# Uneven token parts in the plain dense products of a hybrid decoder layer

## What is computed

```python
z = rmsnorm(x, g_mix_norm) @ w_in             # 2048 -> 8728 columns
u, v, q, kvc, kvs, kvw, g_nsa, g_a, g_b = split_in(z)
o_a = spatial_gate(gelu(u), rmsnorm(gelu(v)))  # 8 groups, causal 128x128 mixing
o_b = nsa(q, kvc, kvs, kvw)                    # compressed + selected + window attention
mix = sigmoid(g_a) * (o_a @ w_proj_gmlp) + sigmoid(g_b) * (o_b @ w_proj_nsa)
x = x + mix @ w_out
hm = rmsnorm(x, g_mlp_norm)
y = x + square(relu(hm @ w_up)) @ w_down
```

## Time and profile before

| | before |
|---|---|
| median of 3 runs | 2601.99 us |
| lowest, highest | 2601.18, 2602.23 us |
| profiled execution, first to last instruction (span) | 2600.4 us |
| TensorE matmuls busy | 2588.5 us, 21487 matmuls |
| weight loads busy | 2560.1 us |
| VectorE, ScalarE, GpSimd busy | 1953.5, 1405.3, 458.6 us |
| granted TensorE clock | 1.00 |
| DMA | 378.79 MB, 146 GB/s on average |

### The profile page before, as it was taken

How to read it: one execution, slowest core, us unless ns; L and a number is a source line. 1 busy time by engine, 2 the same in 40 slices (tenths; PEclk the granted TensorE clock), 3 DMA queues, 4 the chain that set the end, 5 groups by cost and what they waited for, 6 DMA issues and landing times. The chain is left out here.

```text
span 2600.4 us, 57446 instructions
## 1 busy us (share of the span) xinstructions
PE 2588.5 (100%) x21487; PEld 2560.1 (98%) x21487; DVE 1953.5 (75%) x2897; ACT 1405.3 (54%) x2415; POOL 458.6 (18%) x629
## 2 busy tenths in 40 slices
PE   9999999999999999999999999999999999999998
PEld 8999999999999999999999999999999999999998
DVE  6456646668777764455688888888888888898888
ACT  6445436556454442222366666666566665666656
POOL 2001350001121110023202121121121211112113
PEclk9999999999999999999999999999999999999999
DMA  6633552214344344434336575665766756657568
GB/s 212 203 114 114 164 173 74 66 50 132 125 142 137 123 163 138 132 128 145 118 114 159 149 182 144 169 158 149 174 149 167 169 144 166 156 160 175 140 169 180
DMA packets 125325, 378.79 MB, mean 146 GB/s; under 512 B 14258, under 2 KB 15922, under 8 KB 124944
## 3 DMA queue, kind: packets, MB, share of 16 engines
q1 hardware_dynamic: 69328, 245.36, 28.3%
q0 software_dynamic: 52704, 126.25, 22.5%
q10 hardware_dynamic: 3168, 5.45, 0.6%
HBM read 292.29 MB, written 91.00 MB: 147 GB/s over the span
## 5 line engine op out<-in xcount | busy, mean ns | idle before, releaser
L2762 DVE TENSOR_TENSOR w_lo<-w_raw,w_hi 128x1024 fp32r<-128x1024 f32 x351 | 428.0, 1222 | 105.9 <-ACT w_hi L1892 104.5
L1892 ACT ACTIVATE w_hi<-w_raw 128x1024 fp32r<-128x1024 f32 x352 | 370.9, 1062 | 203.0 <-PE aux L1365 69.8
L2069 DVE TENSOR_TENSOR w_lo<-w_raw,w_hi 128x512 fp32r<-128x512 f32 x280 | 202.3, 724 | 340.3 <-ACT w_hi L1510 339.7
L1365 PE MATMUL aux<-at_t,w_hi 128*128 128x260 f32 x2304 | 416.7, 282 | 0.2
L1510 ACT ACTIVATE w_hi<-w_raw 128x512 fp32r<-128x512 f32 x280 | 175.3, 628 | 411.5 <-PE mm L943 391.2
L943 PE MATMUL mm<-a_hi,w_hi 128*128 128x260 f32 x1728 | 357.5, 288 | 0.0
L1365 PEld LDWEIGHTS aux<-at_t,w_hi 128*128 128x128 f32 x2304 | 354.9, 188 | 0.7 <-DVE w_lo L2762 0.3
L1429 PE MATMUL aux<-fb_mid,w_hi 128*128 128x260 f32 x1920 | 352.1, 283 | 1.4 <-DVE w_lo L2762 1.1
L943 PE MATMUL mm<-a_hi,w_lo 128*128 128x260 f32 x1728 | 347.9, 283 | 0.0
L943 PE MATMUL mm<-a_lo,w_hi 128*128 128x260 f32 x1728 | 347.2, 282 | 0.0
L1365 PE MATMUL aux<-at_t,w_lo 128*128 128x260 f32 x1152 | 325.4, 282 | 0.0
(11 more groups left out here) (483 smaller groups left out, 5827.9 us busy)
## 6 DMA issues: line engine op xcount, KB each, us to landing
w_raw<-in_w_ff SPq DMA_DIRECT2D x256, 512.0 KB, 3.5
w_raw<-in_w SPq DMA_DIRECT2D x142, 512.0 KB, 3.5
out_y_t<-y_mid POOLq DMA_DIRECT2D x120, 520.0 KB, 8.0
w_raw<-in_w_st SPq DMA_DIRECT2D x56, 512.0 KB, 3.6
g_in<-merge_d POOLq DMA_DIRECT2D x16, 520.0 KB, 4.9
merge_d<-z POOLq DMA_DIRECT2D x18, 260.0 KB, 4.0
st_f<-in_x_p POOLq DMA_DIRECT2D x8, 520.0 KB, 4.5
pages<-in_cache_cmp POOLq DMA_DIRECT2D x16, 256.0 KB, 4.1
```

The source lines that it names most:

```text
L1365: last = pe.matmul(dst, w, at_t[:, j, e:e + HT], start=FRESH[b] and j == 0 and part == 0, stop=j == KP - 1 and part == 2, skip_group_check ...
L1892: run(hi_of(p, k), source(p, k), ACT.Copy).then_inc(ff_hi, 1)
L2069: dve.tensor_tensor(w_lo[:, c, :], raw(u, c), w_hi[:, c, :].bitcast(F32), ALU.subtract).then_inc(lo_split, 1)
L2762: dve.tensor_tensor(lo_of(p, k), source(p, k), hi_of(p, k).bitcast(F32), ALU.subtract).then_inc(ff_lo, 1)
```

## The change

The tokens of a plain unit are no longer always cut at column 260. A function of the unit's number gives the cut: 260 for units 0 to 3, 256 for 4 to 19, 232 for 20 to 23, 208 for 24 to 27, 260 for 28 to 39, and 256 for 40 to 71 (those of the hardware loops, whose number isn't a Python integer, among them). The first part is written to the last columns of its bank, up to column 511, and the second to the first columns of the next bank, so the 520 sums lie in one run over two banks that are neighbours. VectorE's reads take that run as two pieces of 260 columns. As before, each of a pair's matmuls loads the same weights for itself.

```diff
-        def pair(v):
-            return mm[:, 2 * v:2 * v + 2, 0:HT]
+        def cut_of(n):
+
+            if type(n) is not int or n >= U_PROJ:
+                return 256
+            return HT if n < U_KV else 256 if n < U_VU else 232 if n < U_VU + 4 else 208 if n < U_VU + 8 else HT
+
+        def pair(v, n):
+            o = (2 * v + 1) * 512 - cut_of(n)
+            return mm[:, :, :].rearrange("p b n -> p (b n)")[:, o:o + TOK].rearrange("p (a b) -> p a b", a=2)
+
+        def column_parts(v, n):
+            cut = cut_of(n)
+            return ((mm[:, 2 * v, 512 - cut:512], slice(0, cut)), (mm[:, 2 * v + 1, 0:TOK - cut], slice(cut, TOK)))
...
                         for w, a, part in ((wh, ah, 0), (wh, al, 1), (wl, ah, 2)):
-                            for h in range(2):
-                                last = pe.matmul(mm[:, 2 * v + h, 0:HT], w, a[:, kt, h * HT:(h + 1) * HT],
+                            for dst, cut in column_parts(v, n):
+                                last = pe.matmul(dst, w, a[:, kt, cut],
                                                  start=first and k == 0 and part == 0,
                                                  stop=final and k == CK - 1 and part == 2)
...
-                dve.tensor_tensor(halves(dst), pair(u[1]), halves(rstd[:, :]), ALU.mult).then_inc(mm_read, 1)
+                dve.tensor_tensor(halves(dst), pair(u[1], num(u)), halves(rstd[:, :]), ALU.mult).then_inc(mm_read, 1)
```

More of the change, by code:

```diff
@@ L1020, in first_units @@
                         for w, a, part in ((wh, a_hi, 0), (wh, a_lo, 1), (wl, a_hi, 2)):
-                            for h in range(2):
-                                last = pe.matmul(mm[:, 2 * u + h, 0:HT], w, a[:, kt, h * HT:(h + 1) * HT],
+                            for dst, cut in column_parts(u, 0):
+                                last = pe.matmul(dst, w, a[:, kt, cut],
                                                  start=kt == 0 and part == 0, stop=kt == KT - 1 and part == 2)
@@ L2133, in first_copy @@
                 dve.wait_ge(chunk_done, 2 * CH - 1 + u)
-                dve.tensor_copy(halves(z_first[:, u, :]), pair(u)).then_inc(first_read, 1)
+                dve.tensor_copy(halves(z_first[:, u, :]), pair(u, 0)).then_inc(first_read, 1)
             def first_scale(u):
@@ L2699, in first @@
                         dve.wait_ge(g_loaded[p], 16 * i + 16)
-                        dve.tensor_tensor(halves(ca[:, :]), pair(0), halves(g_in[:, p, 0, :]), ALU.mult
+                        dve.tensor_tensor(halves(ca[:, :]), pair(0, n), halves(g_in[:, p, 0, :]), ALU.mult
                                           ).then_inc(mm_read, 1)
@@ L2704, in _ @@
                     dve.wait_ge(chunk_done, CH * n + CH)
-                    dve.tensor_tensor(halves(cb[:, :]), pair(1), halves(g_in[:, p, 1, :]), ALU.mult).then_inc(mm_read, 1)
+                    dve.tensor_tensor(halves(cb[:, :]), pair(1, n), halves(g_in[:, p, 1, :]), ALU.mult).then_inc(mm_read, 1)
                     dve.wait_ge(mm_read, 2 * n - U_PROJ + 2)
@@ L2745, in x2_sum @@
                 dve.wait_ge(chunk_done, CH * num(u) + CH)
-                dve.tensor_tensor(halves(x2_of(i, p)), pair(p), halves(x2_of(i, p)), ALU.add).then_inc(mm_read, 1)
+                dve.tensor_tensor(halves(x2_of(i, p)), pair(p, num(u)), halves(x2_of(i, p)), ALU.add).then_inc(mm_read, 1)
             for p in range(2):
```

## The result

The changed kernel takes 2606.27 us (median of 18 runs, 2605.09 to 2607.79) against 2602.00 for the kernel before (18 runs beside them): a ratio of 1.0016 with a 95% interval of 1.0009 to 1.0023, some 4.3 us more. The forecast was 2605.4.

What follows compares the result with a forecast made beforehand. TensorE was taken as the bound: the number of matmuls times the spacing of their starts. Only units 20 to 27 cost time, 3.1 to 3.7 us, taken as 3.4: 2602.0 + 3.4 = 2605.4 us, range 2595 to 2614.

Steps and rivals of the forecast that it cites:

- (a): Units 0 to 3 and 28 to 39 keep 260 + 260: cost 0.
- (b): Units 4 to 19 and 40 to 71 at 256 + 264: a pair keeps its 240.3 ns, cost 0.
- (e): VectorE's reads of the run over two banks, one crossing the seam: covered by slack, cost 0.
- (f): Other operand addresses of the moved parts: no sign, 1.1 us either way.
- (c): Units 20 to 23 at 232 + 288: short part waits for its weight load, 3.2 to 4.2 ns more a pair.
- (d): Units 24 to 27 at 208 + 312: short part costs a weight load, 13.2 to 15.0 ns more a pair.
- either bound: A matmul's streaming cost for n columns: n/2.4 + 11.8 ns (fixed), or 0.449 ns a column + 3.5 (by column).
- Rival 1: Every matmul's load and hand-over take 120 ns, not 111.7: 2612 us; chance 0.14.
- Rival 2: Short parts pay nothing, as the engine evens it out over the pair: 2602 us; chance 0.09.
- Rival 3: The 11.8 ns come from where parts begin and end, and new parts avoid them: 2564 us; chance 0.13.
- Rival 4: Short parts in units 20 to 27 run twice at two clocks a column: 2705 us; chance 0.13.
- The Trainium skill's estimate: By the page alone, pairs of 232 + 288 and 208 + 312 cost 7.5 and 17.5 ns more, 4.8 us in all.

Runs made afterwards that it cites:

- a1: The changed kernel with units 20 to 27 cut at 256 too, so no part is under 256 columns: 2602.11 us.
- a2: The changed kernel with 260 + 260 in every unit, the sums still in one run over two banks: 2601.78 us.
- l_232: The changed kernel with 232 + 288 in units 40 to 71 and 260 + 260 in all others: 2608.50 us.
- l_208: The changed kernel with 208 + 312 in units 40 to 71 and 260 + 260 in all others: 2624.07 us.
- l_8: The changed kernel with 8 + 512 in units 40 to 71 and 260 + 260 in all others: 2759.24 us.
- b_step: The changed kernel with 260 + 260 throughout, operands of units 42 to 71 read as every second bfloat16 element: 2589.92 us.
- f_dense: The changed kernel with 260 + 260 throughout, operands of units 42 to 71 read as float16 elements side by side: 2575.79 us.
- h_260: The changed kernel with 260 + 260 throughout, matmuls of units 42 to 71 taking only 64 of 128 weight columns: 2598.34 us.

## Why the prediction was right, and where it was off

- *The bound.* Right: 4.3 of the 4.4 us of span are TensorE's busy time.
- *(a), (b), (e), (f), at nothing.* Right. The merge units have the same 161.47 us, a1 and a2 the time of the kernel before. The reads that cross the seam take 693 and 692 ns against 691 and 692 in the earlier trace rows:

```profile
L2107 DVE TENSOR_TENSOR z<-mm,rstd 128x520 f32<-128x520 f32 x38 | 26.3, 693 | 0.0
L2711 DVE TENSOR_TENSOR na<-mm,g_in 128x520 f32<-128x520 f32 x16 | 11.1, 692 | 0.0
```

- *(c), 3.2 to 4.2 ns a pair.* Too small where it was applied: 5.7 in units 20 to 23, 0.27 us a unit instead of 0.15 to 0.2. In units with nothing between (l_232) it is 4.2, the upper end; where the other 1.5 ns in units 20 to 23 come from was not tested. *(d), 13.2 to 15.0.* 14.8 in units 24 to 27, 14.5 in l_208, inside the bounds. Together (5.7 + 14.8) x 192 = 3.9 us, above the 3.1 to 3.7 of the sum; less the 0.36 us of a wait that became shorter, which the prediction had not seen, 3.57. The forecast took 3.4. That they lie so close is in part luck.
- *The terms behind them.* Two were off and nearly cancelled, which is luck too. The load cycle was taken as 111.7 and is 108.4 to 108.8 ns here; the 110 before matmuls of 7 columns was the better row. The long part costs more than either bound: 146.2 ns for 312 columns (141.8 to 143.6 forecast), 135.6 for 288 (131.8 to 132.8). Behind a late load the parts of 288, 312 and 392 columns pay 2.6 to 3.6 ns above 0.449 ns a column + 3.5, a term that the prediction doesn't have; the part of 512 columns in l_8 pays 1 ns, so it isn't a constant, and its cause is open. Of the two bounds for a column the one by the column is the nearer (l_8), and the middle I took between them was a compromise without a ground.
- *The median.* It grew by 4.3 us and not by 3.4. Of the profiled difference, the scatter of the start makes 0.57 us, as shown above; what it adds to a median of 18 runs isn't known, and the interval (1.0009 to 1.0023, some 2.3 to 6.0 us) holds both figures.
- *Rival 1, a load cycle of 120 ns.* Fallen: 256 + 264 keeps 240.3 ns a pair, and 8 columns cost 108.4. *Rival 2, evened out.* Fallen: l_208. *Rival 3, the parts' ends.* As put, fallen: parts that begin and end on multiples of 32 bytes run at the same 120.1. But its premise, that the excess hangs on how the operand lies in memory, may be right in part: 5 of the 11.8 ns lie between b_step and f_dense. *Rival 4, a least length for one-pass streaming.* Fallen: 8 to 240 columns all run once, at 0.45 ns a column or the load's length. (Its time for a limit between 208 and 232 columns should read 2651: 192 x (253 + 3.7) ns over 2602. And the 2.3 ns that rivals 3 and 4 add to a matmul's columns stands in no row; f_dense has 2.5.)
- *The Trainium skill's estimate.* The Trainium skill ("TensorE: Matmul & The Clock Gate", "LDWEIGHTS (loading the stationary operand)") has 106.7 ns for the load, nearer to the 108.4 measured than my 111.7. Its spacing n/2.4 + 2.5 ("Back-to-back issue gap") is met by f_dense, 110.8 ns, and by no fp32r matmul here. The estimate of 4.8 us worked out from the two figures lies above the 3.9 us that the two groups of units cost, mostly because an even pair, at 221.7 ns, is taken 18.6 ns too cheap and the long parts only 13 to 14.

What stays open: why the pairs of units 20 to 23 pay 1.5 ns more than those of l_232, the 1 to 4 ns that a long part pays behind a late load, and what the streaming's excess is made of.

No kernel here beats the one before with its result intact: h_260 and f_dense leave results out, and b_step, 12.6 us faster, drops the lower halves of its operands' words, at a price in accuracy that is not given here. 260 + 260 is as good as 256 + 264 and 240 + 280.

## What to carry to other kernels

When every matmul loads its own weights, as here (fp32r, 128 weight columns), cutting a tile unevenly is free until the shorter part streams for less time than a load takes, and from there each column moved costs a column's time. Find the two numbers (load to load behind short matmuls, and a long matmul's slope by its columns) before choosing a cut. If matmuls of one shape are the whole time, divide a pure stretch by its count: a gap between that and the clock, here 11%, is worth an experiment on how the operands are read before any work on their order.

## What the hardware showed that I had not expected

- One-pass fp32r streaming doesn't reach one column a clock: 0.45 to 0.46 ns a column at a granted clock of 1.00, against 0.417 at one clock. The excess grows with the columns: 11.8 ns for 260, 21 for 512 (234.4 ns). Of 2-byte elements side by side (f_dense) 260 columns take 110.8 ns, 2.5 over one clock a column.
- 2-byte elements 4 bytes apart (bfloat16) cost 5 ns more for 260 columns than 2-byte elements side by side (float16).
- Full weight loads follow each other 108.4 to 108.8 ns apart beside one-pass parts of 8 to 232 columns.
- Halving the weight load (64 of 128 columns) under a 260-column stream gives 1.4 ns of 120.1.
